# Expert rows by one-hot products at both ends of a sixteen-expert loop

## The reference, cut to what matters

```python
g_logits = (t @ w_group) + b_group
p_g, g_top = lax.top_k(softmax(g_logits), 1)
e_logits = ((t @ w_router) + b_router).reshape(-1, 4, 4)
e_in = jnp.take_along_axis(e_logits, g_top[:, :, None], axis=1)[:, 0]
top_p, top_i = lax.top_k(softmax(e_in), 2)
w = top_p / jnp.sum(top_p, -1, keepdims=True) * p_g
expert_id = g_top * 4 + top_i          # two experts of one group for each token
combine = jnp.sum(jax.nn.one_hot(expert_id, 16) * w[..., None], axis=1)
hid = silu(einsum('td,edf->etf', t, w_gate)) * einsum('td,edf->etf', t, w_up)
y = einsum('etf,efd->td', hid * combine.T[:, :, None], w_down)
x = x + y                              # t is rms_norm(x, norm_ffn_g)
# second block
u = rmsnorm(x, g_pre)
proj = u @ w_in                        # latents, gates, features
```

## Time and profile before

| what | us |
|---|---|
| three runs: median | 1488.93 |
| three runs: lowest, highest | 1482.95, 1491.84 |
| the profiled execution | 1484.55 |
| its span in the trace | 1483.2 |
| TensorE busy | 1381.7 (93%) |
| VectorE, ScalarE, GpSimd busy | 540.1, 348.4, 277.0 |

### The profile page before, as it was taken

The page is one execution under the profiler, slowest core; times in us unless marked ns, Lnnn a source line. Parts: engine busy times, 40 slices in busy tenths (PEclk is TensorE's granted clock), DMA queues, the critical chain, the costliest instruction groups (busy, mean ns, idle before and its releaser), DMA issues. The chain is left out here.

```text
span 1483.2 us, 23489 instructions
## 1 busy us (share of the span) xinstructions
PE 1381.7 (93%) x9996; PEld 740.9 (50%) x9996; DVE 540.1 (36%) x1286; ACT 348.4 (23%) x827; POOL 277.0 (19%) x315
## 2 busy tenths in 40 slices
PE   7998999899999995999999948989999899999997
PEld 4545545565444443444444415446777445655543
DVE  3124423573212534411211114445359482333403
ACT  2125324543101110111111113334221201222221
POOL 3010302204040721122222132010231002111000
PEclk9999999999999996999999978989999999999999
DMA  6154013300312248799999962010140331300311
GB/s 202 57 213 142 1 59 86 142 32 4 113 58 97 104 167 298 271 386 381 381 382 380 380 251 95 8 57 2 57 170 29 73 127 38 123 2 17 115 57 57
DMA packets 99323, 208.15 MB, mean 140 GB/s; under 512 B 14725, under 2 KB 22736, under 8 KB 99088
## 3 DMA queue, kind: packets, MB, share of 16 engines
q1 hardware_dynamic: 87152, 171.38, 32.1%
...
...
## 5 line engine op out<-in xcount | busy, mean ns | idle before, releaser
L454 PE MATMUL pb<-Wt,HT 128*128 128x512 f32 (+1 forms) x384 | 154.7, 561 | 1.3 <-DMA Wt<-in_w_in_dram 1.3
L3416 PE MATMUL pb<-Wt,HT 128*128 128x512 f32 x256 | 117.7, 601 | 0.4 <-DVE AR L3507 0.4
L454 PE MATMUL pb<-Wt,AR 128*128 128x512 f32 x256 | 111.5, 592 | 0.0
L454 PEld LDWEIGHTS pb<-Wt,HT 128*128 128x128 f32 x384 | 71.3, 206 | 71.9 <-issue 71.9
L1952 PE MATMUL pb<-AR 128*64 128x512 f32 x256 | 85.7, 601 | 0.0
L664 PE MATMUL pb<-AR 64*128 64x512 f32 (+7 forms) x256 | 65.5, 501 | 14.1 <-ACT AR L759 4.4
L454 PEld LDWEIGHTS pb<-Wt,AR 128*128 128x128 f32 x256 | 48.1, 190 | 57.9 <-issue 57.9
L3416 PEld LDWEIGHTS pb<-Wt,HT 128*128 128x128 f32 x256 | 46.4, 190 | 51.4 <-issue 48.4
L1952 PE MATMUL pb<-Wt,AR 128*64 128x512 f32 x192 | 70.8, 595 | 0.0
L763 ACT ACTIVATE AR<-AR,SM 128x512 f32<-128x512 f32 (+3 forms) x96 | 53.1, 554 | 51.6 <-DVE SM L715 51.2
L715 DVE CUSTOM_DVE_ANT_0 AR<-pb,AR 128x512 f32<-128x512 f32 (+3 forms) x96 | 43.2, 487 | 57.7 <-PE pb L666 57.4
...
## 6 DMA issues: line engine op xcount, KB each, us to landing
...
```

Of the source, the lines that this page charges most:

```text
L454: r = mm(s[:, 0:n], lT[:, k, t * 128:(t + 1) * 128], w[:, k, c0:c0 + n], start=k == 0, stop=k == nk - 1)
L3416: r = mm(s, HT[:, k, t * 128:(t + 1) * 128], W.ap(("gate2", c, br))[:, k, :], start=k == 0, stop=k == 7)
```

## The change

1. *Ranks in bfloat16.* `MM` and the triangular and ones matrices are bfloat16 tiles; the products for the counts get a bank of their own. The token numbers of `slots` are split in two parts (`ohb`), so that they stay exact: 16 bfloat16 products in place of 8 float32 ones.
2. *Expert 0 without a gather.* VectorE makes `first_p`: for each token tile, 128 x 96, the one-hot of its rank in expert 0 times pick and inverse root mean square. TensorE multiplies `X` with it (32 float32 products of 128x128 by 96 columns, in two halves, `slots` between them) and so gets the turned rows that `turn(0)` made. Later steps run `first_rows(s-1)` ahead of `turn(s)`.
3. *The last two experts stay on the core.* Their rows are not stored but copied to `YA` and `YB_`. One-hot matrices with the weights (`lateA`, `lateB`) are made in step 5 and transposed in step 9. For each token tile four float32 products of 512 columns give what experts 14 and 15 add (`late_rows_pe`); VectorE adds it from PSUM.
4. *Gathers inside the loop.* The eight gathers (`gather_po`) are issued once expert 13's rows are stored. Rows of experts 14 and 15 in `ys` are zero. VectorE adds the gathered rows of tiles 0 and 1 in step 16 ahead of `down(14)`, of tile 2 and half of tile 3 in step 17 ahead of `down(15)`, the last half in the norm.
5. *Loads.* The ring of weight places after the experts begins one place later; the latent weights take expert 14's place. The two loads after them wait for all gathers.

The diff, cut to its core:

```diff
+        LATE = 14
+        ZEROS = LATE * CAP
+        ZROW = OROW + 128 * OV
...
+        W.n = in_slot(("up", 1))
...
-        M1, M2, MM = (small.take(4, 16) for _ in range(3))
+        M1, M2 = (small.take(4, 16) for _ in range(2))
+        MM = picksb[:, :].rearrange("p (t e) -> p t e", e=16)
+        base_t, first_w = small.take(4), small.take(4)
+        first_p = Place(AR, ARN, 16384).take(4, CAP)
...
             vt.tensor_tensor(as_g(MM), *each(e2, oh), ALU.mult).then_inc(s_pick, 1)
+            ve.wait_ge(s_pick, 1)
+            ve.chain(lambda: vt.tensor_tensor(first_w, MM[:, :, 0], norm2.rs, ALU.mult))
...
+            vt.tensor_copy(PO, s).then_inc(P.free("ranks"), 1)
+            ve.wait_ge(*P.drained("ranks"))
+            ve.after()
+            for t in ALLT:
+                r = vt.tensor_scalar(first_p[:, t, :], C["io"][:, 0:CAP], PO[:, t, 0:1], first_w[:, t:t + 1], ALU.is_equal,
+                                     ALU.mult)
+            r.then_inc(s_fpick, 1)
...
+            def first_rows(hf):
+                key = ("xt", 0, hf)
+                ve.wait_ge(*P.filled(key))
+                for i in range(2):
+                    ve.wait_ge(s_spill[i], 32)
+                vt.tensor_tensor(XT[0][:, 4 * hf:4 * hf + 4, :], P.ap(key).rearrange("p (k q) -> p k q", q=128)[:, :, 0:CAP],
+                                 bc(PT[:, 8 + 4 * hf:12 + 4 * hf], CAP), ALU.mult).then_inc(P.free(key), 1)
+            first_rows(0)
             ve.wait_ge(*P.filled("slots"))
             vt.tensor_copy(slots[0:CAP, :], P.ap("slots")[0:CAP, 0:16]).then_inc(P.free("slots"), 1)
+            first_rows(1)
...
+            ve.chain(lambda: vt.tensor_copy(lrank, PO[:, :, LATE:16]))
...
+            for t in ALLT:
+                for e in range(2):
+                    pick = lrank[:, t, e:e + 1], lwt[:, t, e:e + 1], ALU.is_equal, ALU.mult
+                    vt.tensor_scalar(lateA[:, t, 64 * e:64 * e + 64], C["io"][:, 0:64], *pick)
+                    for c in range(2):
+                        o = 64 * c + 32 * e
+                        r = vt.tensor_scalar(lateB[:, t, o:o + 32], C["io"][:, 64:96], *pick)
+            r.then_inc(s_late, 1)
...
-            mm(s[:, 0:64], C["stri"], flatm, start=True, stop=True)
+            flatm = picksb[:, :]
+            r = mm(s[:, 0:64], strib[:, :], flatm, start=True, stop=True)
             for j in range(1, 4):
-                mm(s[:, 16 * j:64], C["ones"], flatm[:, 0:64 - 16 * j], start=False, stop=True, skip_group_check=True)
+                r = mm(s[:, 16 * j:64], onesb[:, :], flatm[:, 0:64 - 16 * j], start=False, stop=True, skip_group_check=True)
+            r.then_inc(P.full("ranks"), 1)
+            s = P.take(pe, "O", "counts")
             for j in ALLT:
-                r = mm(s[:, 64:80], C["ones"], MM[:, j, :], start=False, stop=True, skip_group_check=True)
-            r.then_inc(P.full("ranks"), 1)
+                r = mm(s[:, 0:16], onesb[:, :], MM[:, j, :], start=j == 0, stop=j == 3)
+            r.then_inc(P.full("counts"), 1)
+            def first_rows(hf):
+                pe.wait_ge(s_fpick, 1)
+                s = P.take(pe, "T", ("xt", 0, hf))
+                for j in range(4):
+                    k = 4 * hf + j
+                    for t in ALLT:
+                        r = mm(s[:, j * 128:j * 128 + CAP], X[:, t, k * 128:(k + 1) * 128], first_p[:, t, :], start=t == 0,
+                               stop=t == 3)
+                r.then_inc(P.full(("xt", 0, hf)), 1)
+            first_rows(0)
             s = P.take(pe, "O", "slots")
             for i in range(8):
                 pe.wait_ge(s_oneh, i // 4 + 1)
-                r = mm(s[0:CAP, 0:16], ohp[:, i, :], ohb[:, i, :], start=i == 0, stop=i == 7)
+                for k in range(2):
+                    r = mm(s[0:CAP, 0:16], ohp[:, i, :], ohb[:, k, i, :], start=i == k == 0, stop=i == 7 and k == 1)
             r.then_inc(P.full("slots"), 1)
+            first_rows(1)
...
-                for stage, b in ((turn, step), (first_rows, step - 1), (hidden_turn, step - 2), (last_rows, step - 1),
+                for stage, b in ((first_rows, step - 1), (turn, step), (hidden_turn, step - 2), (last_rows, step - 1),
                                  (down, step - 2)):
-                    if 0 <= b < 16:
+                    if 0 <= b < 16 and (stage, b) != (turn, 0):
                         stage(b)
                     if stage is hidden_turn and step == 4:
                         places_pe()
                     if stage is hidden_turn and step == 6:
                         over_count(pe)
+                    if stage is hidden_turn and step == 9:
+                        late_turn_pe()
...
+        def gathered_ve(t):
+            ve.wait_ge(s_comb[t], 32)
+            for j in range(2):
+                add_ve(t, j)
 
...
-                for stage, b in ((turn, step), (first_rows, step - 1), (last_rows, step - 1), (down, step - 2)):
-                    if 0 <= b < 16:
+                for stage, b in ((first_rows, step - 1), (turn, step), (last_rows, step - 1), (down, step - 2)):
+                    if 0 <= b < 16 and (stage, b) != (turn, 0):
...
+                    if step == 16 and stage is last_rows:
+                        gathered_ve(0)
+                        gathered_ve(1)
+                    if step == 17 and stage is last_rows:
+                        gathered_ve(2)
+                        ve.wait_ge(s_comb[3], 32)
+                        add_ve(3, 0)
...
+                if b >= LATE:
+                    for i in range(2):
+                        ac.wait_ge(s_yst[i], 32 * 3 * (LATE // 2))
+                    for c in range(2):
+                        o = 64 * (b - LATE)
+                        r = st.copy(YA[c][o:o + 64, :], P.ap(("ya", b))[64 * c:64 * c + 64, :])
+                    r.then_inc(P.free(("ya", b)), 1)
+                    ac.wait_ge(*P.filled(("yb", b)))
+                    for i in range(2, 4):
+                        r = st.copy(*last_quarter(b, i))
+                    r.then_inc(s_ycopy, 1)
...
+            pipe(blocks, fetch, None, None, lambda b: store(b) if b < LATE else None)
+            gather_po()
+        def gather_po():
+            po.wait_ge(s_row, 1)
+            for i in range(2):
+                po.wait_ge(s_yst[i], 32 * 3 * (LATE // 2))
+            po.wait_ge(*P.filled(("gb", 14)))
+            po.wait_ge(*P.filled(("yb", 12)))
+            for t in ALLT:
+                for j in range(2):
+                    at = bass.IndirectOffsetOnAxis(ap=rowi[:, j, t:t + 1], axis=0)
+                    gt.indirect_dma_start(g2[t][j], None, ys_dram, at).then_inc(s_comb[t], 16)
 
 
...
+        def late_rows_pe(t):
+            for name in ("lateA", "lateB"):
+                pe.wait_ge(*P.drained(name))
+            for b in (14, 15):
+                pe.wait_ge(*P.drained(("ya", b)))
+            s = [P.take(pe, late_rings[t][c], ("late", t, c)) for c in range(2)]
+            for c in range(2):
+                mm(s[c], lateA[:, t, :], YA[c], start=True, stop=False)
+            for b in (14, 15):
+                pe.wait_ge(*P.drained(("yb", b)))
+            for c in range(2):
+                k = slice(64 * c, 64 * c + 64)
+                mm(s[c], lateB[k, t, :], YB_[k, :], start=False, stop=True).then_inc(P.full(("late", t, c)), 1)
+        late_rings = ("OO", "SS", "ST", "OO")
+        def late_rows_ve(t):
+            for c in range(2):
+                key, x = ("late", t, c), X[:, t, 512 * c:512 * c + 512]
+                ve.wait_ge(*P.filled(key))
+                if c == 0:
+                    ve.after()
+                vt.tensor_tensor(x, P.ap(key), x, ALU.add).then_inc(P.free(key), 1)
+            for c in range(2):
+                ve.wait_ge(*P.drained(("late", t, c)))
 
         def latent_norm_pe():
 
+            for t in range(3):
+                late_rows_pe(t)
             norm3.turn_pe(0)
+            late_rows_pe(3)
...
+            for t in ALLT:
+                sy.wait_ge(s_comb[t], 32)
```

133 lines of the change are left out of this document (98 added, 35 removed).

## The result

The changed kernel took **1476.69 us** (median of 7 runs, 1471.20 to 1479.44) beside 1483.67 us for the kernel before (7 runs on the same chip). The ratio is 0.9942, 95% interval 0.9922 to 0.9961: 8.6 us faster, 5.8 to 11.6. The forecast was 1474 within 1465 to 1483. None of those 24 runs (1479.97 to 1492.94 us) is as fast as the slowest of the seven here. That, more than the number, is what the experiments had to explain.

The account below looks back on a forecast made before the run. TensorE was taken to bound the kernel, idle only in two gaps around the expert loop. 5.1 - 0.3 - 1.2 + 9.4 = 13.0 us gave 1471.5 or 1475.9 by scale; forecast the middle, 1474, range 1465 to 1483.

Parts of the forecast that it names:

- First gap: Routing to expert 0's last rows: one-hot products replace the gather, 5.1 us gained, bounds 0.8 lost to 5.8 gained.
- The rival with a low clock: Routing: the clock stays low through the one-hot products, that part gives -0.8, sum 7.1, 1480 us; chance 9%.
- `hidden_turn(1)` with 0.9 us to spare: Loop, step 2: VectorE's rows ready at 625.7, TensorE asks at 626.6, so nobody waits; 0.3 us charged, bounds 0 and 2.
- The loop: Expert loop: 0.3 us charged for VectorE's later chain in step 2 and 1.2 us lost by `late_turn` in step 9.
- `first_rows` ahead of `turn` moves no sum: Expert loop: the new order keeps the same eight transposes, and the gather is wanted 7 us later.
- The 1.2 us for `late_turn`: Loop, step 9: eight transposes on TensorE's path, 0.95 us, and 0.3 us for banks `turn(9)` just filled; bounds 0.9 and 2.
- Second gap: Behind expert 15: early gathers and late products bring tile 1's transposes to 890.8 against 900.21, 9.4 us gained.
- the bound of 4 us: Behind expert 15: the gain there is only 4 us if VectorE is 5 us late with the gathered rows.
- The port rival: Gathers: three issues wait 1.28 us each for VectorE's adds, last pair 3.8 us later, sum 9.2, 1478 us; chance 13%.
- The slower case: Experts 14 and 15: late gathered rows delay copies and hold TensorE; losing needs the last pair at 884, not 869.6; 3%.
- the text's own sign of being wrong: Loop's end: the forecast is wrong if TensorE idles inside experts 14 and 15; no size given.
- Its low end: Whole kernel: 1465 us, from best bounds 5.8 and 11, less 1.2, on the lower scale.

Follow-up runs that it names:

- those 24 runs: The changed kernel, unedited, measured again on chips 5 and 1: ratios to the kernel before 1.0013 and 0.9987.
- The undoing: The changed kernel with expert 0's rows again by gather and transposes, bfloat16 ranks and the rest kept: ratio 0.9986, on another chip.
- e6: The changed kernel with unread products of constants filling TensorE's waits in the routing: 1483.84 us, against 1487.67 unedited in the same group.
- e4: The kernel before with only `first_rows` put ahead of `turn` in each loop step: 7.5 us slower than before.
- e3: The changed kernel with the overflow slots' products moved behind `last_rows(3)` and the late experts' transposes behind `down(7)`: ratio 0.9928.
- e1: The changed kernel with VectorE's adds for tiles 2 and 3 behind expert 15's copies instead of ahead: ratio 0.9935.
- e12: e11 with the eight gathers held until expert 15's last product and all their adds behind its copies: 1478.67 us.
- e13: e11 with the third and fourth gather pairs waiting for the first and second to land, and three loads later: 1471.81 us, ratio 0.9906.
- e11: The changed kernel with bank tenants moved, adds behind the last two experts' copies and routing waits filled: 1477.06 us.

## Why the prediction was right, and where it was not

- **First gap, 5.1 forecast, 6.0 measured** (5.7 with the longer wait for the picks, of which the forecast charged 0.2). The mechanism and the working hold: one-hot products 2.1 us behind the ranks (2.3 taken), clock back 4.4 us after their start (4.2 taken), records of 96 columns hardly dearer than those of 16 (0.112 us each at full clock, 0.107 reckoned). The undoing gave 6.4. The rival with a low clock did not come about in the products themselves; the half that ran low costs 2.25 us, as e6 shows.
- **`hidden_turn(1)` with 0.9 us to spare, 0.3 charged.** TensorE did not wait there. Right.
- **The loop, 1.5 us of loss forecast, 2.8 measured.** Here the step failed that said "`first_rows` ahead of `turn` moves no sum". It moves PSUM banks: with expert 4's product of gate and up and `turn(5)` ahead of the overflow slots' copy on VectorE, `hidden_turn` waits 1.70 us for that bank, and a further 0.72 stands in the step before. 2.4 us of waits were missed, and 1.6 us of gain too (eleven steps shorter by 0.15), which is luck and not working: e4 shows that the order makes it, and no run shows how. The 1.2 us for `late_turn` were 1.8 (17.31 to 19.09), 1.0 of transposes and 0.72 for the bank.
- **Second gap, 9.4 forecast, 6.4 measured.** The start was put 2.0 us behind expert 15 and came after 3.96: the third pair landed later than reckoned, and its adds stand ahead of the copies, as the bound of 4 us said. The floor under it, 2.3 to 2.65 us over the overflow test, was in no row of before, since 21.61 us of idleness covered it. And the sum took full clock for the late products, though the same text had read that the clock falls in gaps; that is the 3.0 us that e3 and e1 show. One thing was cheaper than reckoned: the four 64-row records of `lateB` took 1.13 us, the four of 128 rows 1.98, so a tile was 2.97 us and not 3.43. No run takes the late rows away; by e12 the gain hangs on the early gathers, for without them it is 56.7 us from expert 15's end to `z_b`, and before it was 53.5.
- **The port rival** did not come about in the result's run. The issues beside VectorE's adds took 0.94 and 0.99 us there, like those without (0.94 to 1.02); in e13 three such took 1.47, 1.02 and 1.08, and in e3 one, which lies wholly beside adds, 1.96. A lock for a whole VectorE operation, as the Trainium skill has it for the two-port modes (SBUF — State Buffer, "Who interferes with whom"), would have cost about 1.3 us each; these rows show 0 to 1.0, so it is no rule here that every such issue waits, and what makes one wait stays open.
- **The slower case, 3%.** It named the right place and the wrong mechanism. It asked for a last pair that lands 14 us later than reckoned (at 884 and not 869.6), so that copies hold TensorE. Gathers that land in time are enough, if ScalarE and TensorE stall while they are issued and under way: 4.4 us in the loop in e11 against e12, and a longer wait behind expert 15. On chips 5 and 1 that, with the clock's falls, ate the gain, and the text's own sign of being wrong, a TensorE that idles inside experts 14 and 15, is seen there. "A transfer that comes late would be felt" was the warning in the first paragraph; the price of eight gathers upon other engines was never bounded, though the 0.27 of transfers in that stretch was to be filled (it became 0.90 in the result's run). The range of the text holds the result; on chips 5 and 1 the measured times, 1487.67 and 1484.84, lie outside it. Its low end does not come out of its terms: 1484.55 less 5.8 and 11, with 1.2 of loss, is 1469 and not 1465.

So the sum of 13.0 was too large by 3.0 (second gap) and 1.3 (loop) and too small by 0.9 (first gap), which makes the 9.6 measured between the ranks and `z_b`. The forecast was right in its side and its range on the chip of the result. That errors of 3.0 and 1.3 one way met 0.9 the other is luck, and so in part is the chip: what the forecast did not know is as large as what it forecast.
